# Modulation rows dealt out 1, 3, 4, 4 in the feed forward's second product, and the pair of score products between the two directions of the inverse levels

## The reference, cut to what matters

```python
mod_x = jnp.split((jax.nn.silu(c) @ w_ada[l] + b_ada[l])[:, None, :], N_MOD, axis=-1)
mod_c = jnp.split((jax.nn.silu(c_ctx) @ w_ada[l] + b_ada[l])[None, None, :], N_MOD, axis=-1)
def swiglu(x, w_in, w_out):
    gate, up = jnp.split(x @ w_in, 2, axis=-1)
    return (jax.nn.silu(gate) * up) @ w_out
xs = ffn_half(xs, mod_x[0], mod_x[1], mod_x[2], g[0], g[1], w_ff_in[l, 0], w_ff_out[l, 0])
cs = ffn_half(cs, mod_c[0], mod_c[1], mod_c[2], g[0], g[1], w_ff_in[l, 0], w_ff_out[l, 0])
```

```python
def step(S, inp):
    r_t, w_t, k_t, v_t, kk_t, a_t = inp
    s_kk = jnp.einsum('bhij,bhj->bhi', S, kk_t)
    S = (S * w_t[:, :, None, :]
         - s_kk[..., None] * (a_t * kk_t)[:, :, None, :]
         + v_t[..., None] * k_t[:, :, None, :])
    return S, jnp.einsum('bhij,bhj->bhi', S, r_t)
```

## Time and profile before

| | us |
|---|---|
| median of 3 runs | 1883.62 (1883.36 to 1883.65) |
| the profiled execution | 1884.41 |
| its span, first to last instruction | 1882.5 |
| TensorE matmuls busy in the span | 1693.7 (90%) |
| VectorE busy | 917.7 (49%) |
| ScalarE busy | 316.5 (17%) |
| GpSimd busy | 166.3 (9%) |

### The profile page before, as it was taken

How to read it: one execution, slowest core, us unless ns; L and a number is a source line. 1 busy time by engine, 2 the same in 40 slices (tenths; PEclk the granted TensorE clock), 3 DMA queues, 4 the chain that set the end, 5 groups by cost and what they waited for, 6 DMA issues and landing times.

```text
span 1882.5 us, 30756 instructions
## 1 busy us (share of the span) xinstructions
PE 1693.7 (90%) x12632; PEld 1355.2 (72%) x12632; DVE 917.7 (49%) x1856; ACT 316.5 (17%) x732; POOL 166.3 (9%) x159
## 2 busy tenths in 40 slices
PE   8999999899999999999999999999999666655656
PEld 3888888899888989779999998887787221211213
DVE  4766666887886466754676135854422000000000
ACT  2200000011210001532111114433313000000001
POOL 3000000001124410001000012640000000000000
PEclk9999999999999999999999999999999877887888
DMA  9344433665763204236545864203299999999996
GB/s 382 142 134 134 130 127 114 252 238 182 289 245 112 83 31 160 68 108 228 191 165 174 294 207 151 72 26 113 90 364 357 428 433 434 431 430 432 434 431 289
DMA packets 47466, 428.36 MB, mean 228 GB/s; under 512 B 5403, under 2 KB 6140, under 8 KB 16252
## 3 DMA queue, kind: packets, MB, share of 16 engines
q1 hardware_dynamic: 37584, 389.07, 53.5%
q10 hardware_dynamic: 9772, 37.69, 5.8%
HBM read 425.69 MB, written 1.05 MB: 227 GB/s over the span
## 4 chain that ended last, share of the span: by engine, by line
PE 31%; DMA 19%; DVE 3%; issue 2%; ACT 1%; POOL 1%; POOLq 0%; SPq 0%; ACTq 0%
DMA arena<-experts_ring_dram 19%; PE bank L1085 11%; PE bank L1269 6%; PE bank L1731 3%; PE bank L2133 2%; PE bank L1598 1%; PE bank L1817 1%; PE bank L1808 1%; PE bank L1929 0%; PE bank L1977 0%; PE bank L1648 0%; POOL rstd L956 0%; PE bank L1752 0%; DVE arena L3503 0%; PE bank L2122 0%
## 5 line engine op out<-in xcount | busy, mean ns | idle before, releaser
L1085 PE MATMUL bank<-arena 128*128 128x128 f32 (+1 forms) x2208 | 354.1, 322 | 0.9 <-ACT arena L2665 0.5
L1085 PEld LDWEIGHTS bank<-arena 128*128 128x128 f32 x2208 | 324.3, 191 | 28.6 <-issue 1.8
L2133 PE MATMUL bank<-arena 128*32 128x512 f32 x1400 | 215.5, 771 | 143.5 <-DMA arena<-experts_ring_dram 143.5
L2133 PEld LDWEIGHTS bank<-arena 128*32 128x32 f32 x1400 | 58.5, 136 | 293.8 <-issue 293.7
L1219 PE MATMUL bank<-arena 128*128 128x256 f32 x880 | 193.9, 379 | 0.0
L1219 PEld LDWEIGHTS bank<-arena 128*128 128x128 f32 x880 | 167.1, 190 | 23.1 <-issue 0.5
L1269 PE MATMUL bank<-arena 128*128 128x128 f32 x1456 | 162.9, 275 | 0.0
L1269 PEld LDWEIGHTS bank<-arena 128*128 128x128 f32 x1456 | 162.8, 192 | 0.1
L3782 DVE TENSOR_TENSOR arena<-arena,bank 128x512 f32<-128x512 f32 x8 | 5.5, 689 | 238.9 <-PE bank L2133 238.9
L1315 PE MATMUL bank<-arena 128*128 128x128 f32 x880 | 102.7, 275 | 0.0
L1315 PEld LDWEIGHTS bank<-arena 128*128 128x128 f32 x880 | 100.7, 192 | 0.2
(11 more groups left out here) (538 smaller groups left out, 2476.3 us busy)
## 6 DMA issues: line engine op xcount, KB each, us to landing
arena<-dense_dram SPq DMA_DIRECT2D x169, 1024.0 KB, 4.9
arena<-experts_ring_dram SPq DMA_DIRECT2D x41, 4096.0 KB, 27.0
arena<-ada_rest_dram ACTq DMA_DIRECT2D x56, 512.0 KB, 3.9
arena<-experts_dram SPq DMA_DIRECT2D x18, 1024.0 KB, 8.7
arena<-ada_head_dram SPq DMA_DIRECT2D x8, 1024.0 KB, 23.1
arena<-experts_dram SPq DMA_DIRECT2D x10, 512.0 KB, 9.3
arena<-tokens_dram ACTq DMA_DIRECT2D x1, 2048.0 KB, 20.8
arena<-experts_ring_dram SPq DMA_DIRECT2D x1, 2048.0 KB, 23.7
```

The costliest lines, as they stand in the source:

```text
L1085: ins = mm(out, lhsT=w, rhs=rhs(k), start=k == 0, stop=k == k_tiles - 1)
L2133: ins = mm(ps[banks[half]][32 * e:32 * e + 32, :], lhsT=lhs[:, 2 * kp + par, CAP * e:CAP * e + CAP], rhs=slab[e][par][:, half * 512:half * ...
```

## The change

Two edits, each in the lists of several engines.

1. A function `out_rows(p)` gives the modulation rows of output pair p for r = 0: 0, then 1 to 3, 4 to 7, 8 to 11, so one, three, four and four, in place of three each. Both VectorE's `ada_late` and ScalarE's `ada_late_loads` go by it. The rows with two products (0 to 3) so fall one to pair 0 and three to pair 1, where before it was three and one.
2. `pair_products` loses its division into halves, with the same matmuls in the same order within a pair. In the levels it moves from behind the two-quarter products to between `four_quarters(0)` and `four_quarters(1)`, and `pair_masked` moves on VectorE from the end of the level to its beginning, ahead of both subtractions. The one exception is level 5 of s = 1, where both stay where they were.

```diff
+def out_rows(p):
+    return ((0, 1), (1, 4), (4, 8), (8, 12))[p]
...
-            def pair_products(s, p, half):
+            def pair_products(s, p):
 
                 d = p // 2 if p < 4 else p - 4
                 ch = d if s == 0 else 1 - d
-                if half == 0:
-                    for b in FILL_BANKS:
-                        take(pe, f"am{s}", b, p)
-                for j in (2 * (p % 2) + half,) if p < 4 else range(2 * half, 2 * half + 2):
+                for b in FILL_BANKS:
+                    take(pe, f"am{s}", b, p)
+                for j in range(2 * (p % 2), 2 * (p % 2) + 2) if p < 4 else range(4):
...
-                for half in range(2):
-                    pair_products(s, 0, half)
+                pair_products(s, 0)
                 for lv in range(1, N_LEV):
                     for d in range(2):
                         pe.wait_ge(nl_ready, s * 2 * N_LEV + lv * 2 + d + 1)
...
                         four_quarters(d)
+                        if d == 0 and not (s and lv == N_LEV - 1):
+                            pair_products(s, lv)
                     for d in range(2):
                         bx = (1, 5)[d]
                         if lv > 1:
                             pe.wait_ge(xt_ready, turned_back(s, lv - 1, d))
                         take(pe, f"inv{s}", bx, lv - 1)
                         two_quarters(d, lv, bx)
-                    for half in range(2):
-                        pair_products(s, lv, half)
-
+
+                if s:
+                    pair_products(s, N_LEV - 1)
                 wanted_values(s)
...
             for p in range(KD // 2):
-                ada_late_loads(3 * p, 3 * p + 3)
+                ada_late_loads(*out_rows(p))
                 out_copy(0, p)
                 out_squared(0, p)
...
                 elif n % OUT_STEPS == 1:
-                    ada_late(3 * p, 3 * p + 3)
+                    ada_late(*out_rows(p))
                     if p:
                         out_squares(0, p - 1)
...
                 pair_masked(s, 0)
                 for lv in range(1, N_LEV):
+                    if not (s and lv == N_LEV - 1):
+                        pair_masked(s, lv)
                     for d in range(2):
...
-                    pair_masked(s, lv)
+                if s:
+                    pair_masked(s, N_LEV - 1)
```

## The result

The changed kernel takes 1873.95 us, median of 5 executions (1872.40 to 1874.71), against 1883.62 (1881.88 to 1883.82): ratio 0.995, with its interval 0.9936 to 0.9965. The forecast was 1873.2. The execution profiled took 1874.70, with a span of 1872.8 us, 9.7 less than the earlier trace rows.

A forecast was written before the change was run, and what follows sets the result against it. TensorE was taken as the bound from the first product to the experts, the tail following it. 6.7 + 3.7 = 10.4 us off the profiled 1884.41, less 0.8 for the median, gave 1873.2; range 1872 to 1875, 8 in 10 1871.5 to 1877.5.

The forecast's parts named there:

- The bound and the tail: Expert loads at the end: every microsecond TensorE reaches them earlier ends the kernel a microsecond earlier; first batch at about 1361.
- Rival 3: Expert tail: its loads are held by something that hasn't moved, so the time stays 1883.6 us; chance 0.03.
- Part one: Second product, line 1315: the 4.60 us wait and the 2.09 us slow restart behind it both go, 6.7 us.
- the loads of the rows: cost 0: ScalarE's queue, second product: moved row loads delay no copy, and weight slabs aren't passed by them; cost 0.
- Pair 1's margin: Second product: VectorE, after three double rows, releases TensorE at 359.0, needed at 359.5; cost 0, bounds 0 and 2 us.
- Rival 2: Second product: the wait moves to pair 1, gain falls to 6 to 9 us, time 1875 to 1878; chance 0.12.
- Part two: Inverse levels: reordering removes three small waits per level, 2.3 us in the first half and 1.4 in the second, 3.7 us.
- the level of 4.39: Inverse levels: 4.84 us less 0.45 us of small waits gives 4.39 us a level, set by TensorE's own issue.
- Rival 1: Inverse levels: the small waits stay or turn into others, only the rows' gain remains, 1876.9 us; chance 0.14.
- VectorE's round: Inverse levels: VectorE's work per level takes 4.15 us, 0.24 below TensorE's 4.39, so it stays hidden.
- rival 4: Inverse levels: VectorE becomes the bound, its round stretched by neighbours' traffic, kernel slower at 1905 us; chance 0.03.
- Nothing behind the levels: Behind the second half's levels: no new wait, as line 1788 already waited 0.24 us for the same subtraction.

The follow-up runs named there:

- rows only: Changed kernel with the level edits undone on TensorE and VectorE, modulation rows still dealt 1, 3, 4, 4; 1875.19 us.
- the pair of the level before: Changed kernel, but each level from 2 on holds the previous level's pair products and masked copies, pair 5 behind the levels in both halves; 1871.76 us.
- the half copies: Changed kernel with each masked copy of pairs 1 to 5 cut to its first half, 128x256 in place of 128x512; 1872.31 us, one execution.
- the masked copy behind: Changed kernel with its TensorE order, but VectorE's masked copies left at the end of the level as before; 1897.47 us, two executions.
- the second profile: Changed kernel run and profiled once more, nothing edited; 1874.52 us, one execution.
- loads behind: Changed kernel, but ScalarE issues pair 3's four row loads behind its copies and squares for that pair; 1873.58 us.

## Why the prediction was right, point by point

**The bound and the tail** (right). TensorE's waits were read from the list, the tail followed: 8.99 us at the issue of the experts (forecast 1361, measured 1362.63), 9.27 at the last load, 9.7 in the span. Rival 3 is excluded. That the median hit so closely is in part luck: see the sum below.

**Part one, the wait and the clock** (right, one term missing). Forecast 6.7. Without the slab wait the product is 6.93 us shorter (129.51 to 122.58): 4.60 of waiting, 2.17 of slow clock (24 records in 2.68 us, I had taken 2.76), 0.16 because the next group starts before the last record ends. The step that failed is "the loads of the rows: cost 0". The sign "line 1315 without a wait over 0.5 us" failed with it, while the granted clock was 1.00 as forecast. I asked whether the row loads would hold up ScalarE's copies, and whether something passes the slabs in a queue. I didn't ask what the fourth load in the burst of pair 3 does to a slab on the other queue, by the bytes alone: the slab took 8.6 us to land in place of 7.3 with three loads. It cost 1.03 us in this execution (0.56 in rows only, with the same order), so part one gave 5.90.

**Pair 1's margin** (right). The sum at 357.05 against 357.4, no wait. Rival 2 is out, with its fellow of pair 3 in its place, a wait for a slab and not for VectorE.

**Part two, the levels** (right in sum, wrong inside). s = 0: 2.41 us against 2.3, s = 1: 1.43 against 1.4. But the level of 4.39 was two misses that cancel, so the agreement of the sum is in part luck, and the sign "levels of 4.3 to 4.5 us" failed. Levels 2 to 5 take 4.14 to 4.17, 0.23 less: two-quarter products that wait for no copy need 1.96 us (1209.48 to 1211.44 by the weight loads), where I had taken 2.17 out of the earlier trace rows. That was the sum of three groups, each to the end of its last load, but the next group begins 0.08 us before that end where nothing holds it:

```profile
1209.48 2.04 PEld L1820 LDWEIGHTS bank<-arena 64*64 64x64 f32 x64
1211.44 0.59 PEld L1811 LDWEIGHTS bank<-arena 64*64 64x64 f32 x32
```

So each small wait had cost more than the idle time that the rows gave it: before, the two-quarter products took 2.55 us to the next group (1214.79 to 1217.34) with 0.32 of idle time in them, after, 1.96 with none.

And level 1 takes 5.22, 0.83 more: the pair needs banks 2 and 6, and I had asked when pair 1's own copies end, not when those of pair 0 do. 0.83 - 4 x 0.23 = -0.09. The kernel with the pair of the level before shows level 1 without that wait and without a pair, 3.85.

**Rival 1 and the rule on bubbles.** The small waits didn't stay: a level fell from 4.84 to 4.14 by order alone, with not one bank or tile more. The Trainium skill, Perfetto Trace Analysis, section Optimization Strategy, reads consistent bubbles as a possible lack of room for the next tile. Here the rows named the copy that each bubble ended at, and the copy was what had to be moved.

**VectorE's round** (right in size, the sign badly chosen). Forecast 4.15 and 0.24 below TensorE; measured 4.14 (1206.54 to 1210.68), level with TensorE, as the level came out shorter. I had called a subtraction right behind the masked copy a sign of rival 4. It did show after, at 1206.54 and 1210.68, and the half copies show that it means nothing yet: two engines with the same round both look like the bound. Rival 4 itself, copies stretched by their neighbours, didn't come: they take 1.33 us as before. What their place can cost is shown by the kernel with the masked copy behind, but by another way: there TensorE waits for the banks, 2.77 us in each level of s = 0 from the second on.

**Nothing behind the levels** (failed). "Behind that nothing new" was said of line 1791, and there it held (0.42 against 0.24 us). The stretch between the halves, which the sum didn't have at all, lost 0.64 us after and 1.43 in the second profile.

In sum 10.4 us were forecast. 1.03 went to the slab and 0.64 between the halves, 0.23 and 0.14 were won on the product and the levels: 9.1, and the experts come 9.0 earlier. The span's 9.7 holds another 0.7 from the tail: 0.3 up to the last load, 0.4 in the last piece of the chain, which scatters by more than that (last section). This 0.7, which no step of the forecast holds, is why the median is only 0.75 above the forecast; in the second profile of the same kernel the experts came 8.3 us earlier, not 9.0. And the range of 1872 to 1875 was tighter than the bounds it was drawn from: 2 us for pair 1 and all 3.7 of part two would have reached to 1879.

## What to carry to other kernels

When work is moved along an engine's list, walk three things at the new place: the engine's own queue, the banks that the moved step needs (who emptied them last, and when), and the bytes that it brings with it, against the transfers of the other queues. Where two engines go through a loop without a gap, shorten one of them, with part of its work left out, before naming the bound. And where medians scatter by more than an edit is worth, compare starts of the same instruction in the traces; over the 735 us between the two places they agreed here to 0.25 us in fourteen traces (735.17 to 735.41), where the median of one change differed from the trace by 2.

## What the runs showed of the hardware

- The clock's fall was all or nothing between two holes at one place: 4.60 us were followed by 24 records in 4.85 us (clock 0.55), 2.11 us by the same records in 2.75 (1.00). Elsewhere, with holes of 2.77 us in four levels, it fell behind the fourth alone (clock 0.51 from 1228.7 to 1232.2).
- A slab of 1 MB landed 4.8 to 4.9 us after its issue with no row load issued just ahead of it (before and loads behind), 7.3 us with three loads of 0.5 MB issued in the 4 us before it on another engine's queue, 8.6 us with a fourth one issued together with it.
- A gap without a releaser on TensorE, 0.46 to 1.23 us, ended 2.2 to 2.7 us behind a 16 KB packet of the instruction queue in eight traces out of eight. Whether the packet is its cause isn't shown.
- The same kernel's slab wait was 0.43 us in one execution and 0.8 in another, and 0.29 to 0.80 over eight traces of the same order. The last piece of the chain, 30.42 us of "issue" after, was 29.0 to 31.0 us over the kernels, which alone moves the time by 2 us, and no edit here touches it. Just ahead of it 64 records of TensorE took 5.38 us at a granted clock of 0.68 after, and 3.69 at 1.00 with the pair of the level before: another 1.7 us that no edit here moved.
